# Loading each block of weights with two transfers of 2 MB in place of four of 1 MB

## The chip, the cores and the metric

The kernel runs on one core of a Trainium2 chip. The metric is the device time of one execution in microseconds (us). Before the change three runs took 2257.77, 2257.80 and 2259.35 us; the median is 2257.8.

## What is computed

A streaming encoder trunk of two layers over 256 tokens of width 2048, all in float32. Each layer is a token mixer, a squared-ReLU MLP with a hidden width of 8192, and a gated embedding, each added to the residual stream `h`; a last RMSNorm closes the trunk.

```python
for i in range(2):
    u = rmsnorm(h, norm_mix[i])
    if i == 0:
        m = conformer_conv_module(u, ...)   # D->2D, GLU, conv of width 31, rmsnorm, silu, D->D (w_pw2)
    else:
        m = short_gated_conv(u, ...)        # D->3D (sc_w_in), gates and a conv of width 3, D->D (sc_w_out)
    h = h + m
    h = h + squared_relu_mlp(rmsnorm(h, norm_mlp[i]), mlp_w1[i], mlp_w2[i])
    h = h + per_layer_embedding(h, p[i], norm_ple[i], ple_w_proj[i], ple_w_gate[i])
return rmsnorm(h, norm_final)
```

## The kernel before

**Blocks, steps, parts.** Behind a front stage of some 240 us that makes the first projection and the wide convolution, all work is a sequence of 92 blocks. A block multiplies the 256 tokens (two groups of 128) with a piece of a weight matrix of 2048 x 512 float32, 4 MB. It has eight steps, e = 0 to 7 (`HALVES = 8` in the code). A step covers 256 rows of the weights: ACT copies them to `whi` in the format fp32r (L586, the high part), DVE subtracts that from the original and gets `wlo` (L927, the low part), and PE makes 12 matmuls with 512 columns (L430 to L432: high by high, high by low, low by high). `whi` and `wlo` have four slots each, so a high part of step e waits until PE has used step e - 4 (`half_used`).

**Loads.** The weights of the next block are fetched into `raw`, which holds exactly one block in four quarters; a quarter is 1 MB and feeds two steps. SP issues the loads (L312). Each has to wait until DVE has made the low parts of the two steps of that quarter in the block before (`lo_ready`, L311), since these read the same bytes. ACT waits for the quarter's semaphore `raw_ready[q]` before the first of its two high parts (L584).

**Results and operands.** Four blocks make a unit: one layer of weights, or a quarter of the MLP's. The units are pw2, then for each layer the MLP as four pairs of an up unit (kind hidden) and a down unit (kind add, the last mlp_out), gate, and between the layers w_in (twelve blocks) and w_out. The result of a block is worked on while PE multiplies the next one. DVE and ACT run their steps in program order: three splits, then `process` of the result and, where it will be the input of a later product, its turning (L1014 and L1016 for hidden, L1008 for the others), then the splits of steps 3 to 7, then the making of the operand (L640, L644 on ACT, L1022, L1028 on DVE). So the low part of the fourth step comes on DVE right behind the turn. The down units but the last, and the last gate, turn nothing. In the second layer's mixer the results of w_in go through taps of the short convolution (L1297, L1299) and L1312 to L1316 instead.

**The way back.** A turned result has to be exchanged between partitions. SP does this by DRAM: four transfers of 128 KB from `turned` to `staged` (L326), a wait for all of them (L328), and one transfer of 512 KB back into `xt`, which lies in `pT` (L336); for w_in's products two transfers into `vpad` (L359). This code is the function `back`, called inside the load of a block behind its first quarter (L319): SP waits for the first quarter's low parts, issues its load, waits for the turn, stages, waits, reads back, and goes on to the second quarter. All of it, the loads too, goes out on SP's one DMA queue. The result of block j is thus carried by the load of block j + 2, which SP works on while PE multiplies block j + 1.

**When an operand is due.** PE uses a unit's results as operands in the next unit that needs them. In its first block (`ready`, L442) every second step waits for one more result; the last of the four is due at the seventh step of that first block, and that is also the block in which it is turned, staged and split.

**The end.** The last block of all is split in another order, 0, 4, 5, 1, 2, 6, 7, 3 (`LAST_ORDER`, L891 and L1346), into buffers that are free by then.

Of the kernel before, what the change touches and what calls it, by code (L numbers as in the profile page):

```python
# [23 lines left out]
P = 128  # L24
EPS = 1e-6
NB = 512
KC = 16
HALVES = 8
TILES = 4
# [71 lines left out]
def trunk(nc, t_in, out):  # L101
    x, p = t_in["x"], t_in["p"]
# [69 lines left out]
    with ctx:  # L172
        def sb(name, shape, dt=F32):
            return ctx.enter_context(nc.sbuf_tensor(name, shape, dt))

        def sem(name):
            return ctx.enter_context(nc.semaphore(name))

        h = sb("h", [P, 2, D])
        raw = sb("raw", [P, TILES, 4, NB])  # L180
# [74 lines left out]

            return acc[:, 2 * (e % 3):2 * (e % 3) + 2, :]

        raw_ready = [sem(f"raw_ready{q}") for q in range(TILES)]
        gate_w = [[sem(f"gate_w{r}{q}") for q in range(TILES)] for r in range(2)]
        val_w = [[sem(f"val_w{r}{q}") for q in range(TILES)] for r in range(2)]  # L260
        wproj_ready, xs_ready = sem("wproj_ready"), sem("xs_ready")
# [11 lines left out]
        hi_ready, lo_ready, half_used = sem("hi_ready"), sem("lo_ready"), sem("half_used")  # L273
# [34 lines left out]
        def _(sp):  # L308
            def tile(b, q, src):

                sp.wait_ge(lo_ready, HALVES * b - HALVES + 2 * q + 2)  # L311
                nc.sync.dma_start(raw[:, q, :, :], src).then_inc(raw_ready[q], 16)  # L312

            def load(b, w, col, row=0, back=None):

                for q in range(TILES):
                    tile(b, q, w[bass.ds(row + q * 4 * P, 4 * P), bass.ds(col, NB)]
                         .rearrange("(c r) n -> r c n", r=P))
                    if q == 0 and back is not None:  # L319
                        back()  # L320
# [18 lines left out]
            def load_unit(unit, w, before, col=0, row=0):  # L339
                for j in range(2):  # L340
                    back = None if before is None else exchange(Result(before, BLOCKS - 2 + j))
                    load(unit.b + j, w, j * NB + col, row, back)
                with sp.Fori(2, BLOCKS) as j:
                    load(unit.b + j, w, j * NB + col, row, exchange(Result(unit, j - 2)))
# [18 lines left out]
            def load_win(next_j, product, gated):  # L363
                for part, first, back in ((0, D, product), (1, 2 * D, gated), (2, 0, None)):
                    load(win.b - 3 + 3 * next_j + part, t_in["sc_w_in"][0], next_j * NB + first - NB, back=back)
# [214 lines left out]
        def _(act):  # L580
            def split_hi(b, e):

                if e % 2 == 0:
                    act.wait_ge(raw_ready[e // 2], 16 * b)  # L584
                act.wait_ge(half_used, HALVES * b + e + 1 - SLOTS)
                nc.scalar.activation(whi[:, e % SLOTS, :, :],  # L586
                                     raw[:, e // 2, 2 * (e % 2):2 * (e % 2) + 2, :],
                                     ACT.Copy).then_inc(hi_ready, 1)
# [59 lines left out]
            def run(b, before=None, after=None, between=None):  # L648

                for e in range(HALVES):  # L650
                    if e == 3 and before:
                        before()
                    split_hi(b, e)
                    if between:
                        between(e)
                if after:
                    after()
# [169 lines left out]
            for e in range(SLOTS):  # L827
                split_hi(pw2.b, e)
# [21 lines left out]
            for i in range(1, UNITS):  # L850
                silu_sigmoid(i)
                silu_hi(i - 1)
                if i <= 2:
                    embedding_out(i + 4)
                if 3 <= i < UNITS - 1:
                    split_hi(pw2.b, i + 1)
                if i == 4:
                    embedding_out(7)
# [27 lines left out]
                run_behind(g1.b + j, Result(g1, j - 1), None)  # L886

            def last_split_hi(b, e):
                act.wait_ge(raw_ready[e // 2], 16 * b)
                act.wait_ge(half_used, HALVES * b + e + 1 - SLOTS if e < SLOTS else HALVES * g1.b)  # L890
                nc.scalar.activation(whi[:, e, :, :] if e < SLOTS else late_hi[:, e - SLOTS, :, :],  # L891
                                     raw[:, e // 2, 2 * (e % 2):2 * (e % 2) + 2, :], ACT.Copy).then_inc(hi_ready, 1)

            r = Result(g1, BLOCKS - 2)
            for e in LAST_ORDER:
                last_split_hi(r.b + 1, e)
# [571 lines left out]
```

## Time and profile before

| | |
|---|---|
| median of three runs | 2257.8 us |
| the profiled execution | 2257.75 us |
| its span, first to last instruction | 2256.0 us |
| busy: PE, PE's weight loads, DVE, ACT, GpSimd | 99%, 83%, 63%, 51%, 7% |
| granted TensorE clock over the span | 0.999 |
| DMA queue q1 (SP's): share of the 16 engines' time | 67.8% |
| chain of work that ended last | PE 98%, DMA 1% |

The span is cut by engine: busy time of an engine is time in which at least one of its instructions ran. A wait is put down to what released it. A DMA instruction of SP only issues; the landing of its data is a separate time. Starts are counted from the start of the span.

### The profile page before, as it was taken

How to read it: one execution, taken by the hardware profiler on the slowest of the kernel's cores; microseconds unless marked ns; L12 is line 12 of the kernel's file. 1: busy time of each engine (PE TensorE's matmuls, PEld its weight loads, DVE VectorE, ACT ScalarE, POOL GpSimd, SP SyncE). 2: the span in 40 equal slices, each digit the busy share in tenths (PEclk: the TensorE clock that was granted, in tenths of full speed). 3: DMA queues.
4: the chain of work that ended last, by engine and by line, in shares of the span. 5: the costliest groups of instructions: out<-in, count | busy, mean ns of one | idle time of the engine just before them, and what ended most of it. 6: DMA issues, size and time to landing. Idle time of an engine off the chain costs nothing.

```text
span 2256.0 us, 29803 instructions
## 1 busy us (share of the span) xinstructions
PE 2236.2 (99%) x10300; PEld 1864.8 (83%) x10300; DVE 1429.1 (63%) x1597; ACT 1145.3 (51%) x1424; POOL 157.1 (7%) x183
## 2 busy tenths in 40 slices
PE   8999999999999999999999999999999999999998
PEld 7998788888888888888888888888888888888886
DVE  6999776555545545566766667665456455556665
ACT  5666555535534534556644444555345345345555
POOL 3888000000000000000000000000000000000000
PEclk9999999999999999999999999999999999999999
DMA  9544477756756856777777677777567567567773
GB/s 340 166 155 145 145 251 256 236 193 206 255 190 196 269 187 204 251 222 256 221 241 220 217 241 213 264 231 253 189 196 267 191 202 252 199 215 224 261 241 112
DMA packets 494098, 494.86 MB, mean 219 GB/s; under 512 B 257936, under 2 KB 296016, under 8 KB 493264
## 3 DMA queue, kind: packets, MB, share of 16 engines
q1 hardware_dynamic: 492192, 491.31, 67.8%
q10 hardware_dynamic: 1696, 1.67, 0.2%
q0 software_dynamic: 144, 1.05, 0.1%
q8 instruction: 36, 0.59, 0.1%
q14 instruction: 30, 0.25, 0.0%
HBM read 460.42 MB, written 33.55 MB: 219 GB/s over the span
## 4 chain that ended last, share of the span: by engine, by line
PE 98%; DMA 1%; DVE 0%; ACTq 0%; issue 0%; ACT 0%; SPq 0%; DVEq 0%
PE acc L430 29%; PE acc L431 29%; PE acc L432 29%; PE acc L492 3%; PE acc L501 2%; PE acc L503 2%; PE acc L502 2%; PE acc L536 1%; PE acc L566 0%; PE acc L565 0%; PE acc L564 0%; DMA emb<-in_cf_b_pw 0%; ACTq L708 0%; DMA staged<-prows 0%; DMA pT<-staged 0%
## 5 line engine op out<-in xcount | busy, mean ns | idle before, releaser
L927 DVE TENSOR_TENSOR wlo<-raw,whi 128x1024 fp32r<-128x1024 f32 x728 | 880.6, 1221 | 590.1 <-ACT whi L586 586.3
L586 ACT ACTIVATE whi<-raw 128x1024 fp32r<-128x1024 f32 x728 | 762.2, 1057 | 774.8 <-PE acc L432 773.8
L430 PE MATMUL acc<-whi,b_hi 128*128 128x512 f32 x1632 | 635.5, 389 | 0.3 <-DVE b_lo L1028 0.3
L432 PE MATMUL acc<-whi,b_lo 128*128 128x512 f32 x1632 | 634.9, 389 | 0.0
L431 PE MATMUL acc<-wlo,b_hi 128*128 128x512 f32 x1632 | 634.9, 389 | 0.0
L430 PE MATMUL acc<-whi,a_hi 128*128 128x512 f32 x1280 | 497.9, 389 | 0.0
L432 PE MATMUL acc<-whi,a_lo 128*128 128x512 f32 x1280 | 497.9, 389 | 0.0
L431 PE MATMUL acc<-wlo,a_hi 128*128 128x512 f32 x1280 | 497.9, 389 | 0.0
L430 PEld LDWEIGHTS acc<-whi,b_hi 128*128 128x128 f32 x1632 | 306.3, 188 | 64.8 <-DVE b_lo L1028 0.7
L432 PEld LDWEIGHTS acc<-whi,b_lo 128*128 128x128 f32 x1632 | 306.3, 188 | 63.8
L431 PEld LDWEIGHTS acc<-wlo,b_hi 128*128 128x128 f32 x1632 | 306.3, 188 | 63.5 <-issue 0.2
L432 PEld LDWEIGHTS acc<-whi,a_lo 128*128 128x128 f32 x1280 | 240.2, 188 | 50.0
L431 PEld LDWEIGHTS acc<-wlo,a_hi 128*128 128x128 f32 x1280 | 240.2, 188 | 49.9
L430 PEld LDWEIGHTS acc<-whi,a_hi 128*128 128x128 f32 x1280 | 240.2, 188 | 49.8
L1187 DVE SCALAR_TENSOR_TENSOR tp<-vpad,vec_rows,tp 128x256 f32<-128x256 f32 x288 | 118.1, 481 | 1.0 <-ACT tp L777 1.0
L501 PE MATMUL acc<-front_x_hi,front_w 128*128 128x256 f32 x330 | 98.8, 299 | 1.2 <-DVE a_hi L1150 1.2
L503 PE MATMUL acc<-front_x_hi,front_w 128*128 128x256 f32 x330 | 93.2, 283 | 0.0
L502 PE MATMUL acc<-a_hi,front_w 128*128 128x256 f32 x330 | 93.2, 282 | 0.0
L492 PE MATMUL acc<-xT,raw 128*128 128x256 f32 x364 | 83.7, 379 | 0.7 <-DVE xT L1135 0.7
L1014 DVE STREAM_TRANSPOSE prows<-res 128x512 f32<-128x512 f32 x32 | 35.2, 1100 | 69.3 <-ACT res L615 69.3
L609 ACT ACTIVATE work<-acc,rinv 128x512 f32 (+1 forms) x64 | 43.6, 681 | 64.9 <-PE acc L432 64.9
L1407 POOL TENSOR_TENSOR res<-work,res 128x256 f32<-128x256 f32 x80 | 75.7, 980 | 0.0
(161 smaller groups left out, 1244.5 us busy)
## 6 DMA issues: line engine op xcount, KB each, us to landing
raw<-in_mlp_w SPq DMA_DIRECT2D x256, 1024.0 KB, 5.5
raw<-in_sc_w_in SPq DMA_DIRECT2D x48, 1024.0 KB, 5.7
raw<-in_cf_w_pw SPq DMA_DIRECT2D x64, 512.0 KB, 8.7
raw<-in_ple_w_gate SPq DMA_DIRECT2D x32, 1024.0 KB, 6.1
staged<-prows SPq DMA_DIRECT2D x240, 128.0 KB, 3.3
pT<-staged SPq DMA_DIRECT2D x56, 512.0 KB, 3.3
raw<-in_cf_w_pw SPq DMA_DIRECT2D x16, 1024.0 KB, 6.8
raw<-in_sc_w_out SPq DMA_DIRECT2D x16, 1024.0 KB, 7.6
```

The source lines that it names most:

```text
L430: nc.tensor.matmul(o, xhi[:, k, s], hi, start=first and c == 0, stop=False)
L431: nc.tensor.matmul(o, xhi[:, k, s], lo, start=False, stop=False)
L432: mm = nc.tensor.matmul(o, xlo[:, k, s], hi, start=False, stop=last and c == 1)
L492: mm = nc.tensor.matmul(o, ring[:, k // 4, k % 4, s:s + P], xT[:, k, :], start=k == 0, stop=k == KC - 1)
L501: nc.tensor.matmul(o, hi, front_x_hi[:, k, :], start=False, stop=False)
L502: nc.tensor.matmul(o, hi, front_x_lo[:, k, :], start=False, stop=False)
L503: mm = nc.tensor.matmul(o, lo, front_x_hi[:, k, :], start=False, stop=k == KC - FULL - 1)
L586: nc.scalar.activation(whi[:, e % SLOTS, :, :], raw[:, e // 2, 2 * (e % 2):2 * (e % 2) + 2, :], ACT.Copy).then_inc(hi_ready, 1)
L609: relu = nc.scalar.activation(zb[:, m:m + 1, :], acc[:, bass.ds(2 * r.pair + m, 1), :], ACT.Relu, scale=rinv[:, m:m + 1])
L927: nc.vector.tensor_tensor(wlo[:, e % SLOTS, :, :], raw[:, e // 2, 2 * (e % 2):2 * (e % 2) + 2, :], whi[:, e % SLOTS, :, :].bitcast(F32), A ...
L1187: ins = nc.vector.scalar_tensor_tensor(o, src, w, o, ALU.mult, ALU.add)
L1407: nc.gpsimd.tensor_tensor(o, made[:, t % 4, :], o, ALU.add).then_inc(made_used, 1)
```

## The change

Each block's weights come in two transfers of 2 MB, each filling two quarters. A transfer waits for the low parts of all four steps whose bytes it overwrites (`lo_ready` two higher than before for the first quarter of the pair). There are two `raw_ready` semaphores in place of four, and ACT waits before steps 0 and 4. The function `back` is still called behind the first transfer. Splits, products and everything else are as they were.

```diff
-        raw_ready = [sem(f"raw_ready{q}") for q in range(TILES)]
+        raw_ready = [sem(f"raw_ready{q}") for q in range(TILES // 2)]
...
-                sp.wait_ge(lo_ready, HALVES * b - HALVES + 2 * q + 2)
-                nc.sync.dma_start(raw[:, q, :, :], src).then_inc(raw_ready[q], 16)
+                sp.wait_ge(lo_ready, HALVES * b - HALVES + 2 * q + 4)
+                nc.sync.dma_start(raw[:, q:q + 2, :, :].rearrange("p q c n -> p (q c) n"), src
+                                  ).then_inc(raw_ready[q // 2], 16)
...
-                for q in range(TILES):
-                    tile(b, q, w[bass.ds(row + q * 4 * P, 4 * P), bass.ds(col, NB)]
+                for q in (0, 2):
+                    tile(b, q, w[bass.ds(row + q * 4 * P, 8 * P), bass.ds(col, NB)]
                          .rearrange("(c r) n -> r c n", r=P))
                     if q == 0 and back is not None:
                         back()
...
-                if e % 2 == 0:
-                    act.wait_ge(raw_ready[e // 2], 16 * b)
+                if e % 4 == 0:
+                    act.wait_ge(raw_ready[e // 4], 16 * b)
...
             def last_split_hi(b, e):
-                act.wait_ge(raw_ready[e // 2], 16 * b)
+                act.wait_ge(raw_ready[e // 4], 16 * b)
```

## Rows read from the trace of the kernel before

**Rows 1.** Page part 1 (busy us, share, instructions of each engine), and who made PE wait

```profile
PE 2236.2 (99%) x10300; PEld 1864.8 (83%) x10300; DVE 1429.1 (63%) x1597; ACT 1145.3 (51%) x1424; POOL 157.1 (7%) x183
...
PE acc L430 <- DVE b_lo L1028: 0.3, 1, 0.3
```

**Rows 2.** ACT's timeline (start, duration, line, out<-in, idle before <-releaser), 698 to 718 us

```profile
708.75 1.06 ACT L586 ACTIVATE whi<-raw 128x1024 fp32r<-128x1024 f32 x1 [1.66 <-PE acc L432]
711.47 1.06 ACT L586 ACTIVATE whi<-raw 128x1024 fp32r<-128x1024 f32 x1 [1.66 <-PE acc L432]
713.94 1.06 ACT L640 ACTIVATE b_hi<-pT 128x1024 f32 x1 [1.42 <-DMA pT<-staged]
```

**Rows 3.** SP's DMA issues in the timeline, 697 to 714 us

```profile
704.92 2.96 SPq L326 DMA_DIRECT2D staged<-prows  x4
710.42 0.34 SPq L336 DMA_DIRECT2D pT<-staged  x1
711.04 3.27 SPq L312 DMA_DIRECT2D raw<-in_mlp_w  x3
```

**Rows 4.** DVE's timeline, 698 to 718 us

```profile
702.44 1.10 DVE L1014 STREAM_TRANSPOSE prows<-res 128x512 f32<-128x512 f32 x1 [2.25 <-ACT res L615]
...
704.80 3.55 DVE L927 TENSOR_TENSOR wlo<-raw,whi 128x1024 fp32r<-128x1024 f32 x3
...
716.33 1.22 DVE L927 TENSOR_TENSOR wlo<-raw,whi 128x1024 fp32r<-128x1024 f32 x1
```

**Rows 5.** Timelines of ACT and of DVE, 774 to 783 us

```profile
779.04 1.06 ACT L640 ACTIVATE b_hi<-pT 128x1024 fp32r<-128x1024 f32 x1 [1.23 <-DMA pT<-staged]
...
780.14 1.23 DVE L1022 TENSOR_TENSOR b_lo<-pT,b_hi 128x1024 fp32r<-128x1024 f32 x1 [1.07 <-ACT b_hi L640]
```

**Rows 6.** Landings of the three L312 issues from 711.04, us after issue

```profile
DMA to landing us min/median/max: 5.5/7.6/8.0
```

**Rows 7.** The DMA queue from 704.9 to 710.4 us: packets, MB, share of 16 engines

```profile
q1 hardware_dynamic: 4160, 0.52, 64.7%
```

**Rows 8.** Page part 6, DMA issues: count, KB each, median us from issue to landing

```profile
raw<-in_mlp_w SPq DMA_DIRECT2D x256, 1024.0 KB, 5.5
...
prows<-in_cf_b_pw SPq DMA_DIRECT2D x1, 256.0 KB, 7.9
```

**Rows 9.** Timelines of DVE and of ACT in an mlp_out block, 983 to 1001 us

```profile
984.01 1.22 DVE L968 TENSOR_TENSOR res<-acc,h 128x1024 f32 x1 [0.94 <-PE acc L432]
...
988.94 3.50 DVE L927 TENSOR_TENSOR wlo<-raw,whi 128x1024 fp32r<-128x1024 f32 x3 [1.43 <-ACT whi L586]
...
999.32 1.23 DVE L927 TENSOR_TENSOR wlo<-raw,whi 128x1024 fp32r<-128x1024 f32 x1 [0.23 <-ACT whi L586]
...
996.62 0.91 ACT L644 ACTIVATE a_hi<-pT,vec_rows 128x256 f32 x2 [1.22 <-DMA pT<-staged]
```

**Rows 10.** DVE's timeline in a pw2 block, 286 to 305 us

```profile
292.97 4.64 DVE L927 TENSOR_TENSOR wlo<-raw,whi 128x1024 fp32r<-128x1024 f32 x4 [1.43 <-ACT whi L586]
```

**Rows 11.** DVE's timeline in a gate block, 1092 to 1108 us

```profile
1093.11 0.69 DVE L987 TENSOR_TENSOR work<-work,emb 128x512 f32<-128x512 f32 x1 [1.19 <-ACT work L624]
...
1097.71 3.45 DVE L927 TENSOR_TENSOR wlo<-raw,whi 128x1024 fp32r<-128x1024 f32 x3
```

**Rows 12.** DVE's timeline in a w_in block, 1157 to 1178 us

```profile
1158.12 1.41 DVE L1271 SCALAR_TENSOR_TENSOR res<-acc,rinv,work 128x512 f32<-128x512 f32 x2 [0.34 <-PE acc L432]
...
1161.68 2.33 DVE L927 TENSOR_TENSOR wlo<-raw,whi 128x1024 fp32r<-128x1024 f32 x2
...
1171.28 1.14 DVE L1297 TENSOR_SCALAR work<-vpad,vec_rows 128x256 f32<-128x256 f32 x4
...
1175.76 2.35 DVE L927 TENSOR_TENSOR wlo<-raw,whi 128x1024 fp32r<-128x1024 f32 x2
```

**Rows 13.** Stretches at the end: us, busy us of each engine, PEclk, DMA share, GB/s

```profile
2246.00:2250.00 4.00, 0.08 (x1) 0.00 (x0) 2.79 (x8) 2.89 (x6) 0.00 (x0) 1.00 0.00 0
2250.00:2256.00 6.00, 0.00 (x0) 0.00 (x0) 1.38 (x5) 0.94 (x1) 0.00 (x0) 0.52 0.44 175
```

## The prediction

> **What bounds the kernel now.** I read the busy shares first: PE works 2236.2 of the span's 2256.0 us [rows 1]. Then who makes PE wait: inside the long stretch of weight blocks only one wait, 0.3 us, for an operand's low part made at L1028 [rows 1]. So the kernel runs at PE's pace, and a change can cost time only where it makes PE wait; there is almost nothing to win.
>
> The pace is read from ACT. In steady work a high part (L586) starts when PE gives back a slot, once in each of a block's eight steps: 708.75 and 711.47, so 2.72 us a step and 21.76 us a block [rows 2]. The one at 711.47 is the eighth of its block and waits for PE's fourth step, so PE began this block at 711.47 - 4 x 2.72 = 700.59. Call that moment T0; other blocks' T0 lie whole multiples of 21.76 away (the w_in blocks apart, where the work at L1271 marks it).
>
> What matters next is the way of a result back to an operand: DVE turns it (L1014/L1016 or L1008), SP writes it to `staged` in four transfers and reads it back as `xt`, ACT and DVE make the operand's parts after the eighth split of the block, and only then split the next block's first quarter. In the block at 700.59: staging issued at 704.92, read back issued at 710.42 [rows 3], ACT's operand part at 713.94 [rows 2], the next block's first low part ending at 717.55 [rows 4]. PE needs that at 722.35: 4.8 us of slack. Where the result is the unit's fourth, the next unit already multiplies and needs the operand at its seventh step: T0 = 765.87 (three blocks on), so at 782.19, and it is ready at 780.14 + 1.23 = 781.37 [rows 5]. Slack 0.8 us.
>
> **The change, step by step.** 368 loads of 1 MB become 184 of 2 MB. SP is idle most of the time, so half its issues save nothing. Where no result goes back (the down units but for their first block, two of three w_in blocks), the first transfer is issued when the fourth low part ends and is needed at T0 + 13.6, the second is issued when the eighth ends (T0 + 13.2) and is needed at T0 + 24.5. A 2 MB load takes about 8.0 us (next paragraph), landing by about T0 + 10.7 and T0 + 21.4: hidden, cost nothing.
>
> How long 2 MB takes is not in the trace; bounds. Of three 1 MB loads issued at 711.04, about 711.7 and 713.95 [rows 3], the landings come 5.5, 7.6 and 8.0 us after issue [rows 6]: 716.5, 719.3, 721.9, so 2.7 us a megabyte when they queue. The first, right behind a read back, takes 5.5; with nothing ahead I take 5.3. So 5.3 + 2.7 = 8.0; below it the two spacings with no lead at all, 5.4, above it two loads in full, 10.6. I take 8.0, since it uses spacing and lead as this queue shows them.
>
> Now the blocks with a result going back, 60 of them (240 staging transfers at four each). Before, the first quarter's load waited for two low parts, was issued before the block began and was gone when staging came. Now it waits for the fourth low part, which DVE makes after the turn, and SP's staging stands behind it in program and in the queue. In the block at 700.59 the fourth low part ends at 706.0 (the first of three from 704.80) [rows 4]. Then: 0.16 to the issue; 8.0 for 2 MB; then the staging, whose packets filled the 16 engines for 64.7% of 5.5 us = 3.5 us [rows 7]; then 3.5 from the read back's issue to ACT's start (710.42 to 713.94). Sum K = 15.2 us. ACT's operand part starts at 721.2 in place of 713.94, 7.2 late. The tail to the first low part, 717.55 - 713.94 = 3.6, puts that at 724.8; PE goes on at 724.9 in place of 722.35. **Cost 2.5 us.**
>
> That staging really stands behind the load is the step on which all hangs. The nearest row is the 256 KB of `prows`, issued by SP right behind weight loads: 7.9 us to land, longer than the usual 1 MB load (5.5) [rows 8]. So small transfers wait for big ones ahead in this queue. The Trainium skill says the same mechanism (DMA: Bandwidth & Descriptors, "Queues, rings and completion order": each engine consumes one ring's descriptors in order, and interleaves only between rows); by that rule, with all of this on SP's row, the staging waits in full, as here.
>
> After such a stall DVE has a backlog: PE starts as the first low part ends, and the second and third (1.2 us each) end 2.4 us into the block. Steps of the next result that began earlier move there.
> - **Hidden results, 8 units.** First result 2.5. Second and third: the turn at L1014 moves from 702.44 [rows 4], 1.85 us in, to 2.4, so 0.5 later, 3.0 each. Fourth: fourth low part at T0 + 5.2, ACT at +20.4, operand complete 2.3 later (781.37 - 779.04) [rows 5] at 22.7 against the seventh step's 16.3: 6.4, with backlog 6.8. A unit 15.3, eight 122.
> - **mlp_out twice, w_out.** T0 = 983.47; L968 at 984.01, fourth low part ends 990.16 = T0 + 6.7, tail 996.62 to 1000.55 = 3.9 [rows 9]. 6.7 + K + 3.9 + 0.1 = 25.9: 4.1. With backlog L968 starts 1.8 later: 5.9 twice. Fourth: low part at about 7.7, operand at 7.7 + 15.2 + 2.3 = 25.2: 8.9. A unit 24.8, three 74.
> - **pw2.** T0 = 287.15, fourth low part ends 294.2 = 7.05 [rows 10]: 4.5. With backlog the bias addition (L980, as wide as a low part, so 1.2) moves behind it too, 2.8 later: 7.3 twice, fourth 10.7. Together 30.
> - **gate, first layer.** T0 = 1092.27; L987 at 1093.11, fourth low part ends 1098.9 = 6.6 [rows 11]: 4.0; with 1.5 of backlog 5.5 twice; fourth 9.1. Together 24.
> - **w_in.** The product's turn: L1271 at 1158.12, fourth low part ends 1162.87, 4.75 on; two read backs, 3.9; then twelve taps from 1171.28 before the low part that ends at 1176.97, 5.7 [rows 12]. 4.75 + 0.16 + 8.0 + 3.5 + 3.9 + 5.7 + 0.1 = 26.1: 4.4. The other turn of each round, with backlog, about 5.0; in w_out's first block it is due at the seventh step, 8.1. Together 4 x 4.4 + 3 x 5.0 + 8.1 = 41.
> - **The last block** splits its fifth part second, and that comes with the second transfer: about 1.
> - Sum 122 + 74 + 30 + 24 + 41 + 1 = 292 us.
>
> **TensorE's clock.** Before, PE never rests. At the end it does: the granted clock is 1.00 to 2250, 4 us after the last matmul, then 0.52 [rows 13], 2.4 and 1.2 GHz. Stalls of 2.5 to 3 us are shorter than that; the 14 stalls at a seventh step (6.8 to 10.7) are longer, so I expect the low level when PE goes on. If it lasts for all 5.44 us of the two steps left, each costs 5.4 more; if the clock doesn't fall, nothing. No row shows how fast it returns: I take the middle, 2.7, 14 times, 38 us (0 to 76). Inside a chain of stalled blocks a slow start is absorbed, because the transfers and not PE set the period.
>
> **Sum.** 292 + 38 = 330 on the profiled execution's 2257.75 (span 2256.0 and 1.75 around it), which is also the median of 2257.8: **2588 us**, +14.6%.
>
> A rule that bears on the size: the Trainium skill (DMA: Bandwidth & Descriptors, "Anatomy of one DMA — SWDGE (gpsimd) path") fits a transfer as 2.0 us plus bytes at 436 GB/s, for the other issuing path. That makes 2 MB 6.8 us, 1.2 less in each of 60 blocks, and the sum 2516; the same page's "Rules for kernel authors" recommends at least 1 MiB per transfer and coalescing, which here is met before the change.
>
> **Rivals.**
> - *The clock stays up.* The stalls are as above but PE restarts at full level: 2258 + 292 = 2550. For it: the only fall seen came after a final stop. Chance 0.24.
> - *The queue shares its engines.* Staging packets go between the load's. Then staging takes at most twice its 3.5 us: read back about 4.7 us late for hidden results in place of 7.2, which the 4.8 us hides except at the seventh step (4 x 8 = 32), and some 75 elsewhere: about 2365. Against it: [rows 8]. Chance 0.09.
> - *Not slower.* The staging is delayed, but less than the seventh step's slack. It decides at 0.8 us; SP's issue alone moves from 704.92 to about 706.8, 1.9 us, so it needs the tail to shrink too. 2258. Chance 0.02.
> - *It cascades.* The second transfer, issued only after the read back, lands too late for the fifth step (I have it 1 us early), or the longer stalls' slow clock is not absorbed: 40 to 100 more, 2630 to 2690. Chance 0.1.
>
> The forecast itself, then, 0.55. **Range**: the bounds for 2 MB, 2.6 us to either side, would be 156 us over 60 blocks; spacing and lead are both seen, so I let K be off by 1.5 us down and 1.2 up. From 2550 - 90 = 2460 to 2588 + 72 = 2660. Cases outside it (sharing, no loss, K further off, the worst cascade) hold about 0.19. A change under 0.2% can't be told from none here: faster 0.01, same 0.01, slower 0.98.
>
> **What the profile after would show.** PE waits on L927's low parts and on b_lo/a_lo (L1022, L1028) of some 290 us in all; a read back landing about 20.4 us after T0 for hidden results; 2 MB landing in about 8 us; staging's last transfer landing 10 us or more after issue in place of 3.4; PE's clock low behind the seventh-step stalls only. If staging lands within 5 us of issue, the queue step is wrong; if the waits are right but the time isn't, the clock step.

## The result, and the profile after

The changed kernel takes **2550.9 us** (median of 4 runs, 2549.6 to 2552.3) against 2257.8: a ratio of 1.130 [1.128, 1.131], 293 us more. Its profiled execution took 2552.3, 2550.5 of it the span. In its code every line below the edit stands one line further down than before (L927 is now L928).

The page of the changed kernel, its busy times, the granted clock in 40 slices, the chain that ended last, and the DMA issues (count, KB, median us from issue to landing):

```profile
PE 2327.9 (91%) x10300; PEld 1913.9 (75%) x10300; DVE 1416.4 (56%) x1597; ACT 1132.0 (44%) x1424; POOL 157.1 (6%) x183
...
PEclk9999989999999999999899999999999999999989
...
PE 32%; SPq 17%; DMA 15%; DVE 10%; issue 6%; ACT 5%; DVEq 1%; ACTq 0%
...
raw<-in_mlp_w SPq DMA_DIRECT2D x128, 2048.0 KB, 8.1
...
staged<-prows SPq DMA_DIRECT2D x240, 128.0 KB, 8.1
pT<-staged SPq DMA_DIRECT2D x56, 512.0 KB, 3.3
```

PE was busy 99% of the span [rows 1], now 91%. The chain no longer belongs to PE: SP's queue and DMAs hold a third of it. 1 MB took 5.5 us to land [rows 8], 2 MB take 8.1, and the 128 KB staging transfers also take 8.1.

Who makes PE wait, in the changed kernel (us in total, times, longest):

```profile
PE acc L431 <- DVE wlo L928: 120.0, 45, 5.3
PE acc L431 <- DVE a_lo L1023: 22.8, 4, 5.7
PE acc L431 <- DVE b_lo L1023: 21.2, 4, 5.9
PE acc L431 <- DVE b_lo L1029: 20.5, 3, 7.6
PE acc L431 <- DVE a_lo L1029: 14.1, 2, 7.8
PE acc L431 <- DVE a_lo L1317: 3.8, 1, 3.8
```

Before, the last row of [rows 1] was all there was: 0.3 us. The first row here is a block's first low part, the others are operands due at a seventh step. Together 202 us. I also lined the two kernels up by the first matmul of each of the 92 blocks: up to the last block's start 294 us are new, 202 of stalls and 92 that the matmuls themselves take longer, because the clock was granted at half in 39 stretches (a 40th lies behind the last matmul, as before the change).

**One stalled block.** PE began it at 763.48 (T0): its wait ends at 787.72, less the 2.48 us of that wait and the 21.76 of eight steps. SP's and ACT's timelines (start, duration, line, out<-in, and idle time before with its releaser):

```profile
769.13 0.37 SPq L312 DMA_DIRECT2D raw<-in_mlp_w  x1
769.70 8.36 SPq L327 DMA_DIRECT2D staged<-prows  x4
780.50 0.35 SPq L337 DMA_DIRECT2D pT<-staged  x1
781.04 0.38 SPq L312 DMA_DIRECT2D raw<-in_mlp_w  x1
```

```profile
774.39 1.06 ACT L587 ACTIVATE whi<-raw 128x1024 fp32r<-128x1024 f32 x1 [1.66 <-PE acc L433]
783.92 1.06 ACT L641 ACTIVATE b_hi<-pT 128x1024 f32 x1 [8.47 <-DMA pT<-staged]
```

DVE's and PE's, same block:

```profile
767.73 3.55 DVE L928 TENSOR_TENSOR wlo<-raw,whi 128x1024 fp32r<-128x1024 f32 x3
...
785.17 1.23 DVE L1023 TENSOR_TENSOR b_lo<-pT,b_hi 128x1024 f32 x1 [8.46 <-ACT b_hi L641]
786.31 3.49 DVE L928 TENSOR_TENSOR wlo<-raw,whi 128x1024 fp32r<-128x1024 f32 x3
```

```profile
787.72 0.49 PE L431 MATMUL acc<-whi,a_hi 128*128 128x512 f32 x1 [2.48 <-DVE wlo L928]
788.04 0.39 PE L432 MATMUL acc<-wlo,a_hi 128*128 128x512 f32 x1
...
789.67 0.63 PE L431 MATMUL acc<-whi,a_hi 128*128 128x512 f32 x1
```

The fourth low part, the first of the three from 767.73, ends at about 768.9; the 2 MB load is issued at 769.13. The four staging issues, 2.96 us long in [rows 3], now take 8.36, the read back goes out at 780.50, ACT starts the operand at 783.92 after 8.47 us without work, and PE stands still for 2.48. From 768.9 to 783.92 is 15.0: the K of the prediction (15.2). Behind the stall the matmuls start 0.23 us apart, then from 788.8 on 0.42 (last section).

What the queue moves in that time: DMA views of two stretches, from just behind the load's issue and from just ahead of its landing (packets, those under 512 B, and by queue):

```profile
DMA packets 548, 1.12 MB, mean 321 GB/s; under 512 B 0, under 2 KB 0, under 8 KB 548
...
q1 hardware_dynamic: 548, 1.12, 100.9%
```

```profile
DMA packets 1819, 0.34 MB, mean 227 GB/s; under 512 B 1761, under 2 KB 1761, under 8 KB 1819
```

The load's packets have 2 KB (1.12 MB in 548), the staging's 128 B (0.52 MB in the 4160 of [rows 7]). From 770.5 to 774.0 (first view) none is under 512 B, though two staging transfers were issued at 769.7 and 770.3; from 776.0 to 777.5 (second view) 1761 are. The small transfers move when the 2 MB are nearly through.

### The profile page after: what moved, and what is told of

It reads as the page before. It is cut to its first block, busy times and chain, and to the rows that moved or that the text cites. A ratio compares the mean times of both kernels' runs of the same rounds, so it can differ in the third digit from the quotient of the medians.

```text
span 2550.5 us, 29149 instructions
## 1 busy us (share of the span) xinstructions
PE 2327.9 (91%) x10300; PEld 1913.9 (75%) x10300; DVE 1416.4 (56%) x1597; ACT 1132.0 (44%) x1424; POOL 157.1 (6%) x183
## 4 chain that ended last, share of the span: by engine, by line
PE 32%; SPq 17%; DMA 15%; DVE 10%; issue 6%; ACT 5%; DVEq 1%; ACTq 0%
SPq L327 16%; PE acc L431 11%; PE acc L432 10%; PE acc L433 10%; DMA staged<-prows 7%; DMA pT<-staged 7%; DVE wlo L928 6%; ACT whi L587 1%; SPq L312 1%; DVE prows L1015 1%; DVE prows L1017 1%; ACT b_hi L641 1%; ACT a_hi L641 1%; DVE res L969 1%; DMA vpad<-staged 1%
## 5 line engine op out<-in xcount | busy, mean ns | idle before, releaser
L928 DVE TENSOR_TENSOR wlo<-raw,whi 128x1024 fp32r<-128x1024 f32 x728 | 873.3, 1221 | 557.3 <-ACT whi L587 554.5
L587 ACT ACTIVATE whi<-raw 128x1024 fp32r<-128x1024 f32 x728 | 751.6, 1054 | 753.0 <-PE acc L433 753.0
L431 PE MATMUL acc<-whi,b_hi 128*128 128x512 f32 x1632 | 656.0, 402 | 107.3 <-DVE wlo L928 65.6
L432 PE MATMUL acc<-wlo,b_hi 128*128 128x512 f32 x1632 | 650.1, 398 | 0.0
L433 PE MATMUL acc<-whi,b_lo 128*128 128x512 f32 x1632 | 649.2, 398 | 0.0
L431 PE MATMUL acc<-whi,a_hi 128*128 128x512 f32 x1280 | 516.7, 404 | 95.1 <-DVE wlo L928 54.4
L432 PE MATMUL acc<-wlo,a_hi 128*128 128x512 f32 x1280 | 512.3, 400 | 0.0
L433 PE MATMUL acc<-whi,a_lo 128*128 128x512 f32 x1280 | 510.8, 399 | 0.0
L1023 DVE TENSOR_TENSOR a_lo<-pT,a_hi 128x1024 f32 (+1 forms) x16 | 19.6, 1226 | 122.6 <-ACT a_hi L641 122.6
L1023 DVE TENSOR_TENSOR b_lo<-pT,b_hi 128x1024 f32 (+1 forms) x16 | 19.6, 1226 | 117.7 <-ACT b_hi L641 117.7
L1029 DVE SCALAR_TENSOR_TENSOR b_lo<-pT,vec_rows,b_hi 128x256 f32 (+1 forms) x48 | 20.2, 482 | 103.8 <-ACT b_hi L645 103.8
```

The costliest lines, as they stand in the source:

```text
L431: nc.tensor.matmul(o, xhi[:, k, s], hi, start=first and c == 0, stop=False)
L432: nc.tensor.matmul(o, xhi[:, k, s], lo, start=False, stop=False)
L433: mm = nc.tensor.matmul(o, xlo[:, k, s], hi, start=False, stop=last and c == 1)
L587: nc.scalar.activation(whi[:, e % SLOTS, :, :], raw[:, e // 2, 2 * (e % 2):2 * (e % 2) + 2, :], ACT.Copy).then_inc(hi_ready, 1)
L928: nc.vector.tensor_tensor(wlo[:, e % SLOTS, :, :], raw[:, e // 2, 2 * (e % 2):2 * (e % 2) + 2, :], whi[:, e % SLOTS, :, :].bitcast(F32), A ...
```

## The experiments

Each was run beside the kernel before; a ratio is to that. Where a kernel has transfers of unequal size, `tile` takes their number of quarters n as well, waits for `2 * q + 2 * n` low parts and loads n quarters, and the tuples (q, n) tell the kernel.

**e3, the second pair alone as one transfer.** Against the kernel before:

```
-                for q in range(TILES):
+                for q, n in ((0, 1), (1, 1), (2, 2)):
```

> Quarters 0 and 1 as two transfers of 1 MB with the waits of before, quarters 2 and 3 as one of 2 MB behind the eighth low part. Theory: nothing of it stands ahead of a staging, and the 2 MB land 3 us before their first split: 2258 to 2262 us. Rival (late weights or size): between 2300 and 2550 us.

Measured 2258.5, ratio 1.0004 [0.9994, 1.0013]. Its page, busy times and issues:

```profile
PE 2237.6 (99%) x10300; PEld 1865.2 (83%) x10300; DVE 1429.2 (63%) x1597; ACT 1145.3 (51%) x1424; POOL 157.1 (7%) x183
...
raw<-in_mlp_w SPq DMA_DIRECT2D x64, 2048.0 KB, 8.2
...
staged<-prows SPq DMA_DIRECT2D x240, 128.0 KB, 3.3
```

A transfer of 2 MB that nobody stands behind costs nothing, for all its 8.2 us, and three issues a block in place of four gain nothing.

**e4, the first pair alone.**

```
-                for q in range(TILES):
+                for q, n in ((0, 2), (2, 1), (3, 1)):
```

> Quarters 0 and 1 as one transfer of 2 MB behind the fourth low part, then quarters 2 and 3 as two of 1 MB with the waits of before. Theory: the whole loss, within 10 us of the changed kernel: 2541 to 2561 us. Rival (the second transfer has a part in it): clearly less, 2400 to 2500 us.

Measured 2551.7, ratio 1.131 [1.129, 1.133]. Its staging lands 8.1 us after issue again and its PE waits add up to 208 us. The whole loss lies in the first transfer.

**e2, the later waits without the larger transfers.** Four of 1 MB, held back as the change holds its two:

```
-                sp.wait_ge(lo_ready, HALVES * b - HALVES + 2 * q + 2)
+                sp.wait_ge(lo_ready, HALVES * b - HALVES + (4 if q < 2 else 8))
```

> Four transfers of 1 MB as before the change, but each waits as the 2 MB ones do: the first two for the fourth low part, the last two for the eighth. Theory: the staging stands behind 1 MB instead of 2, 2.7 us less in each block with a way back; from the excesses measured by block (hidden 2.5, 2.2, 1.7, 8.2; mlp_out and w_out 4, 5, 5, 10; pw2 5.5, 6.6, 6.6, 13.8; gate 5, 5, 5, 10; w_in 44 in all) each less 2.7 and not below 0: 2258 + 142 = 2400 us, give or take 25. Rival (size alone, the waits are harmless): 2258 us. Rival (the wait alone): 2550 us.

Measured 2396.4, ratio 1.061 [1.059, 1.063]: 139 us, as the theory had it (2400), and neither rival's time. Now 1 MB stands ahead of the staging. Its page's issues:

```profile
staged<-prows SPq DMA_DIRECT2D x240, 128.0 KB, 5.8
```

**e6, the wait with no load ahead.** The kernel before, with SP waiting for the fourth low part ahead of the staging (`mark` is a semaphore that nobody waits for):

```
                     if q == 0 and back is not None:
+                        sp.wait_ge(lo_ready, HALVES * b - HALVES + 4)
+                        nc.sync.sem_inc(mark, 1)
                         back()
```

> The kernel before, with one wait added: SP also waits for the fourth low part before it stages, with no load issued in between (one increment of a spare semaphore carries the wait). Theory: staging comes 1.2 us later for hidden results, 2.5 us for most others; the first three results of a unit have 3.2 to 5 us of slack, so only seventh steps wait: 0.5 us in 8 of them, 1 to 2 in six: 2258 + 13 = 2271, 2263 to 2285 us. Rival (the later staging, and not the load ahead of it, is most of the loss): 2400 us or more.

Measured 2281.0, ratio 1.010 [1.009, 1.012]: 23 us, 10 more than the theory's point and far from the rival's 2400. SP's later start costs that much, and behind the same wait for the fourth low part 0, 1 and 2 MB ahead of the staging make it 23, 139 and 293.

**e11, 3 MB ahead.** The same order with three quarters in the first transfer, which waits for the sixth low part: `for q, n in ((0, 3), (3, 1))`.

> The order of the changed kernel, with quarters 0 to 2 in one transfer of 3 MB behind the sixth low part, and the last quarter in one of 1 MB. Theory: every way back comes 2.7 us (1 MB more ahead of it) and 2.3 to 2.4 us (two low parts more to wait for) later than in the changed kernel, 5 us in each of 60 blocks, nothing of it hidden any more: 2551 + 300 = 2851 us, 2815 to 2885. Rival (the loss is the clock's and the wait's, not the queue's): at most 2551 + 60 x 2.4 = 2695 us.

Measured 2929.1, ratio 1.296 [1.294, 1.299]: 671 us, 78 more than reckoned. Its timelines of SP, ACT and PE in one block that began at 841.84:

```profile
850.14 0.37 SPq L312 DMA_DIRECT2D raw<-in_mlp_w  x1
850.71 11.16 SPq L327 DMA_DIRECT2D staged<-prows  x4
864.37 0.35 SPq L337 DMA_DIRECT2D pT<-staged  x1
```

```profile
867.74 1.06 ACT L641 ACTIVATE b_hi<-pT 128x1024 f32 x1 [13.63 <-DMA pT<-staged]
```

```profile
871.53 0.79 PE L431 MATMUL acc<-whi,a_hi 128*128 128x512 f32 x1 [7.64 <-DVE wlo L928]
```

The first hidden results cost 7.4 to 8.7, near what was reckoned (7.5), the second and third about 10 and 9 against 7, the seventh steps 15 to 16 against 13.2. Here the clock is at half for 567 us in all up to the last matmul, against 198 in the change. The sixth split waits for a slot that PE gives back in its second step, so a slow PE delays the next load; in the change the fourth low part waits for no slot of the running block. That this is where the 78 went was read from the trace, not tried.

**e1, the read back's work ahead of the first load.** The changed kernel with two calls exchanged:

```
                 for q in (0, 2):
-                    tile(b, q, w[bass.ds(row + q * 4 * P, 8 * P), bass.ds(col, NB)] ...
                     if q == 0 and back is not None:
                         back()
+                    tile(b, q, w[bass.ds(row + q * 4 * P, 8 * P), bass.ds(col, NB)] ...
```

> The change as it is, but SP does the way back (staging and read back) ahead of the first 2 MB transfer instead of behind it. Theory (the staging stands behind the load): hidden results' read back is issued 9.8 us into the block as before, the 2 MB go out at 10.5 and land at about 13.2 + 5.4 = 18.7, the next block's first low part ends at about 21 where 21.7 is due, so hardly any wait: 2258 to 2270 us. Rival (a 2 MB transfer as such brings the weights too late, or costs in the queue): still over 2500 us.

Measured 2329.8, ratio 1.031 [1.029, 1.033]: three quarters of the loss are gone, but 72 us stay, where I had expected none. Its timelines of SP, ACT and PE, one block:

```profile
548.34 0.35 SPq L337 DMA_DIRECT2D pT<-staged  x1
549.04 3.28 SPq L312 DMA_DIRECT2D raw<-in_mlp_w  x2
```

```profile
560.96 2.95 ACT L587 ACTIVATE whi<-raw 128x1024 fp32r<-128x1024 f32 x3 [8.09 <-DMA raw<-in_mlp_w]
```

```profile
563.46 0.79 PE L431 MATMUL acc<-whi,a_hi 128*128 128x512 f32 x1 [3.15 <-DVE wlo L928]
```

Both loads are now issued behind the read back, at 549.04 and 551.95, and land at 560.85 and 566.00: 11.8 and 14.1 us. The first split of the next block waits for the first. The DMA view of 557 to 567, share of the 16 engines in 40 slices:

```profile
DMA  9999999999999999998642111211100000000000
```

A share of 0.1 is about two engines; under one in ten stands as 0. In the last 2 us before 566.00 one or two engines of 16 are busy, then none: the load's slowest engine sets its landing.

**e5, e9, e10: the same exchange with other sizes.** e5 is the kernel before with `back()` ahead of its first 1 MB; e9 has ((0, 1), (1, 1), (2, 2)), e10 ((0, 2), (2, 1), (3, 1)), both with `back()` first.

> The kernel before, with SP doing the way back ahead of the first 1 MB transfer. The run with the way back ahead of 2 MB lost 72 us because its transfers, two of 2 MB in flight together, landed 8.4 to 14 us after issue and so too late for the next block's first part. Theory (that loss is one of size: a first part waits for 2 MB and for the slowest engine of them): the first 1 MB is issued at about 10.5 us into the block and lands at 16, 1.5 us later than its first part is split now, inside 4.8 us of slack: 2257 to 2263 us. Rival (any load put behind the read back costs): 2300 us or more.

> The way back first, then two transfers of 1 MB and one of 2 MB (the second pair). Behind the read back the 2 MB transfers of the earlier run landed 8.0 to 11.8 us after issue, issued at 10.5 us into the block where PE needs the first low part at 21.7. Theory (late is the first part's own transfer, because it is 2 MB): with 1 MB first it lands 5.5 to 6 us after issue, and the time is that of four 1 MB transfers with the way back first, 2263 us, or a little more for a late fifth part: 2258 to 2275 us. Rival (what counts is all that is in flight, 4 MB): 2320 us or more.

> The way back first, then one transfer of 2 MB and two of 1 MB. Theory (the first part's own transfer is late because it is 2 MB): most of the 72 us that the way back first lost with two transfers of 2 MB: 2305 to 2340 us. Rival (the second 2 MB made the loss): under 2280 us.

Measured 2263.2 (ratio 1.0027 [1.0017, 1.0037]), 2267.6 (1.0043 [1.0026, 1.0060]) and 2337.7 (1.035 [1.033, 1.037]). Each theory's range held, e5's at its upper edge. So with the read back out of the way a second pair in one transfer costs at most some 4 us over e5, which the runs hardly separate (their intervals overlap). 2 MB in the first place cost 62 (e1 against e9) to 75 (e10 against e5): what e1 still loses is its first transfer landing late.

**e8, the first 2 MB on another queue.** The changed kernel, from the first MLP on; SP keeps its wait but adds one to `mark` in place of issuing, GpSimd issues the load on its own queue, and ACT waits for `pool_ready` before step 0:

```
+                pool.wait_ge(lo_ready, HALVES * b - HALVES + 4)
+                nc.gpsimd.dma_start(raw[:, 0:2, :, :].rearrange("p q c n -> p (q c) n"), src).then_inc(pool_ready, 16)
```

> The changed kernel with the first 2 MB transfer of each block issued by GpSimd on its own queue (from the first MLP on), SP waiting for the same fourth low part before it stages as now. Theory (the staging stands behind the load because both are in one ring): the two share the engines, the staging takes at most twice its 3.5 us, the read back comes some 3.5 to 4.5 us earlier than now, and the time falls to about 2370 us (2330 to 2420). Rival (each engine serves transfers in the order of issue whatever the queue): 2550 us.

Measured 2610.7, ratio 1.157 [1.155, 1.159]: 60 us slower than the change, where I had expected most of the loss to go, and slower than the rival's 2550 too. Page and SP's timeline in one block (GpSimd's issue in it is at 827.77, landing at 837.25):

```profile
raw<-in_mlp_w POOLq DMA_DIRECT2D x64, 2048.0 KB, 9.4
...
staged<-prows SPq DMA_DIRECT2D x240, 128.0 KB, 9.6
```

```profile
827.30 7.39 SPq L333 DMA_DIRECT2D staged<-prows  x4
839.17 0.35 SPq L343 DMA_DIRECT2D pT<-staged  x1
```

The DMA view of 834 to 836 us, by queue (packets, MB, share of 16 engines):

```profile
q0 software_dynamic: 186, 0.76, 95.2%
q1 hardware_dynamic: 186, 0.02, 7.6%
```

The engines do serve both queues, 186 packets each. But what they share evenly is the number of packets, and a packet has 4 KB in GpSimd's load (0.76 MB in 186) and 128 B in the staging, so the staging gets 0.02 MB in 2 us. The Trainium skill says the first half of this (DMA: Bandwidth & Descriptors, "Queues, rings and completion order"): an engine goes round the queue rows it has work for at packet granularity. The trace agrees as far as it shows, in equal numbers of recorded packets; the order on a single engine isn't in it.

**e7, PE kept busy in the wait.** The changed kernel with 22 unused matmuls of 512 columns ahead of the wait at the seventh step, in the first block of each of the eight MLP down units (the extra work is added, nothing is left out):

```
                 for e in range(HALVES):
+                    if fill and e == 6:
+                        for i in range(fill):
+                            nc.tensor.matmul(acc[:, 4, :], xhi[:, 0, 0:P], ...
```

> The changed kernel with 22 matmuls of 512 columns more (about 4.8 us, their sums are used by nobody) ahead of PE's wait at the seventh step of each MLP down unit's first block, where PE otherwise stands idle for 5.5 to 7 us. Theory (what these blocks lose beyond their stall is the clock, low for 3.4 to 6.8 us behind it): the clock stays at 1.00 there, and the excess of these 8 blocks falls from 8.3 to about 6.3 us: 2550 - 16 = 2535, 2527 to 2543 us. Rival (the loss has another cause, or matmuls added to the stall cost their own time): 2551 us or more.

Measured 2539.7, ratio 1.125 [1.123, 1.127]: 11 us less than the change, with more work, and inside the theory's range. In these eight blocks the clock doesn't fall, and they take 6.4 us more than before in place of 8.2. Stretches around such a wait (us, busy us by engine, PEclk, DMA share, GB/s), first in the change, then in e7:

```profile
850.00:856.00 6.00, 1.80 (x8) 1.14 (x7) 0.00 (x0) 1.03 (x2) 0.00 (x0) 1.00 0.72 218
856.00:862.00 6.00, 4.59 (x14) 3.72 (x15) 3.50 (x3) 2.11 (x4) 0.00 (x0) 0.72 0.64 245
```

```profile
850.00:856.00 6.00, 5.33 (x24) 4.07 (x24) 3.50 (x3) 2.96 (x3) 0.00 (x0) 1.00 1.01 384
856.00:862.00 6.00, 6.00 (x28) 4.99 (x27) 3.36 (x3) 2.13 (x2) 0.00 (x0) 1.00 0.00 0
```

## Why the prediction was right, and by how much it was off

The direction, the mechanism and the range held; the point was 37 us too high. Measured against predicted, in us over the kernel before, by blocks (the predicted seventh steps with their 2.7 of clock):

| | predicted | measured |
|---|---|---|
| hidden results, first to third of 8 units | 68 | 53.7 |
| their seventh steps, 8 | 76 | 65.9 |
| mlp_out twice and w_out, first to third | 47.7 | 43.1 |
| their seventh steps, 3 (two of mlp_out's, one of w_out's unit) | 34.8 | 31.0 |
| pw2 | 32.5 | 32.5 |
| gate, first layer | 26.8 | 24.1 |
| w_in, with the seventh step of w_out's first block | 43.4 | 43.5 |
| last block | 1 | 0.7 |
| sum | 330 | 294 |

- **What hangs on the queue: right.** e3 and e4 put the whole loss on the first transfer, and e6, e2 and the change make it grow with what stands ahead of the staging. The rival that staging shares the engines is out in the change's own packets.
- **K: right.** 15.0 against 15.2 in the block shown: 8.35 us for its 2 MB (median 8.1, predicted 8.0), the staging done 3.0 behind it in place of 3.5, 3.4 from the read back's issue to ACT.
- **The first stall of a hidden unit: right,** 2.48 against 2.5 in the block shown; over the eight units that first block grew by 2.3 to 3.6, 2.7 in the mean.
- **The backlog: mis-sized.** I had the second and third results begin 0.5 us (hidden) or 1.8 (mlp_out) later, because DVE still splits for 2.4 us. I left out that ACT gains: it no longer waits for the previous block's last matmul, which ended before the stall. In the next hidden block L610 starts at T0 itself, not 0.5 behind it, and the fourth low part ends at T0 + 5.24 against 5.4. So second and third cost about 2.2 and 1.7, not 3.0 each, the chains of mlp_out and w_out 43.1 in all, not 47.7, and the seventh steps inherit less.
- **The clock: the right sign, a size too large, and the wrong places.** A seventh step pays 1.8, by e7, not 2.7; if all 14 pay as e7's eight did, that is 13 of the 37. It also falls behind stalls of 2 to 2.5 us, which I had excluded. There it costs nothing of its own in the sum: in the chain the next stall shrinks by what PE lost. Five of the eight hidden units have the fall in their second result's block and three don't; that block grew by 2.18 to 2.34 with it and by 2.13 to 2.37 without. In the block after the one shown PE waits only 0.39 us at its end, having run at half from 788.6 to 792.1, and the period is 24.04 all the same. That is why PE's waits add up to 202 and not to the 290 that I named as a sign, though the time fits.
- **The rival "clock stays up", 2550, has the measured number and the wrong reason:** its stalls were to be 292 us at full clock; the trace has 202 and the rest in slow matmuls.
- **The sharing rival, 2365, was mispriced.** I had let the staging take at most twice its own 3.5 us. e8 makes the queues share, and the staging takes 9.6: what is shared evenly is packets, not time. Even with sharing the loss stays.
- **A sign I named wrongly:** staging's last transfer was to land 10 us or more after issue. The median of all 240 is 8.1, but in the block shown the last is issued only at 777.4 and lands 3.1 later, because SP is held in the second and third issue, 3.63 and 3.36 us. Only the read back's landing tells, 20.3 after T0 (I had 20.4).
- **Fetch size.** The fit of the Trainium skill (DMA: Bandwidth & Descriptors, "Anatomy of one DMA — SWDGE (gpsimd) path") gives an estimate of 6.8 us for 2 MB, and the prediction's sum by it was 2516. The measured time is 2551. The loads measured 8.1 on SP's queue, and 9.4 in e8 on GpSimd's, beside the staging.

## What to carry to other kernels

Before you join two loads, list what stands behind them in the same queue: a small transfer on the way of a result waits for all the bytes ahead of it, here 2.7 us for each MB (1, 2 and 3 MB land 5.5, 8.1 and 10.8 us after issue). Another queue didn't help it in e8, where its packets had 128 B beside 4 KB. A large transfer cost nothing where nobody waited behind it (e3), so if you join any, join those that come last in a period, and let the short, urgent ones go out first. Then ask whether the joined load itself still lands in time: e1 and e10 lost 72 and 80 us because it didn't. No kernel here beat the one before, whose PE is busy 99% of its span.

## What the runs showed of the hardware that was not expected

- **Large loads in flight together land late and unevenly.** Behind a read back the first 2 MB took 8.0 to 11.8 us and the second 10 to 14.8 in e1, where 8.1 is the median in the change. In e10, with two of 1 MB behind them, the first 2 MB took 8.1 to 12.2. The tail of the load shown has one or two engines busy for 2 us. Why these engines lag was not found.
- **Two queues share by packets.** 186 packets against 186 in 2 us, 0.76 MB against 0.02 (e8).
- **An issue can hold its engine for microseconds.** Behind the 2 MB of the change, the second and third staging issue each stand some 3.4 us on SP; the four issues take 8.36 us in place of 2.96. That the queue had no room for their packets would explain it, but no view shows it.
- **TensorE's granted clock falls behind short stalls too.** In windows of the changed kernel around the 2.48 us stall that ends at 787.72:

```profile
785.00:788.00 3.00, 0.52 (x3) 0.29 (x2) 2.83 (x3) 3.00 (x4) 0.00 (x0) 1.00 1.02 346
788.00:789.00 1.00, 1.00 (x5) 0.76 (x5) 1.00 (x2) 0.97 (x3) 0.00 (x0) 0.82 0.70 270
789.00:790.00 1.00, 1.00 (x4) 0.81 (x3) 1.00 (x2) 0.88 (x3) 0.00 (x0) 0.50 0.06 21
...
792.00:793.00 1.00, 1.00 (x6) 0.84 (x5) 0.96 (x1) 0.65 (x1) 0.00 (x0) 0.97 0.00 0
```

The stall is over before the level falls: PE works again from 787.72, is granted 2.4 GHz until about 788.6, then 1.2 until 792.1. It loses 1.75 us there, which this chain of transfers takes in and a seventh step does not.
